# Stationary operands of the wide products stored with high and low words in turn

## The reference

```python
mix = jnp.einsum('btd,de->bte', merged, w_out[l])
...
h = h + _rmsnorm(jnp.einsum('btf,fd->btd', u, w_down[l]), post_mlp_norm[l])
...
def swiglu(x, w_gu, w_down):
    gu = jnp.einsum('bsd,df->bsf', x, w_gu)
    g, u = gu[..., :D_FF_2], gu[..., D_FF_2:]
    return jnp.einsum('bsf,fd->bsd', jax.nn.silu(g) * u, w_down)
...
    for e in range(N_EXPERTS):
        out = out + gates[..., e:e + 1] * swiglu(x, w_gu[e], w_down[e])
```

## Time and profile before

| | |
|---|---|
| median of 3 runs | 1770.74 us (1767.08 to 1770.81) |
| profiled execution | 1766.83 us, of it span 1765.0 us |
| PE busy | 1743.4 us, 99% |
| weight loads | 1571.6 us, 89% |
| DVE, ACT, POOL busy | 1361.9 us, 1076.1 us, 157.7 us |
| granted TensorE clock | 0.996 of full speed |
| read from HBM | 438.99 MB, 251 GB/s over the span |

### The profile page before, as it was taken

The page is one execution under the profiler, slowest core; times in us unless marked ns, Lnnn a source line. Parts: engine busy times, 40 slices in busy tenths (PEclk is TensorE's granted clock), DMA queues, the critical chain, the costliest instruction groups (busy, mean ns, idle before and its releaser), DMA issues.

```text
span 1765.0 us, 26513 instructions
## 1 busy us (share of the span) xinstructions
PE 1743.4 (99%) x11249; PEld 1571.6 (89%) x11249; DVE 1361.9 (77%) x1591; ACT 1076.1 (61%) x1200; POOL 157.7 (9%) x165
## 2 busy tenths in 40 slices
PE   9999999999999999999999999999999999999997
PEld 8999999999988999998998888888888888888885
DVE  6895488677764667656687899888889898889897
ACT  7654455565644454443446777777777777767674
POOL 1454170000000100000030100000000000000110
PEclk9999999999999999999999999999999999999999
DMA  9332364656556555565463699999999999999994
GB/s 290 120 109 72 118 176 136 226 180 194 192 188 203 193 172 172 183 228 187 128 225 112 232 376 378 378 342 384 369 385 339 383 371 383 333 379 375 381 390 171
DMA packets 265206, 447.90 MB, mean 254 GB/s; under 512 B 11461, under 2 KB 135848, under 8 KB 264952
## 3 DMA queue, kind: packets, MB, share of 16 engines
q1 hardware_dynamic: 263464, 440.36, 71.5%
q0 software_dynamic: 1616, 5.77, 0.8%
HBM read 438.99 MB, written 4.73 MB: 251 GB/s over the span
## 4 chain that ended last, share of the span: by engine, by line
PE 90%; DVE 6%; ACT 3%; issue 1%; DMA 0%; SPq 0%; DVEq 0%; ACTq 0%
PE bank L428 27%; PE bank L429 27%; PE bank L430 27%; DVE ring_r L418 3%; PE bank L3240 1%; ACT hi_ring L403 1%; PE bank L3154 1%; PE bank L2522 1%; PE bank L1348 1%; PE bank L1340 1%; DVE arena L923 1%; PE bank L1832 1%; PE bank L2503 0%; PE bank L2152 0%; PE bank L1817 0%
## 5 line engine op out<-in xcount | busy, mean ns | idle before, releaser
L418 DVE TENSOR_TENSOR ring_r<-ring,hi_ring 128x2048 fp32r<-128x2048 f32 x401 | 905.4, 2285 | 260.8 <-ACT hi_ring L403 260.5
L403 ACT CAST hi_ring<-ring 128x2048 fp32r<-128x2048 f32 (+1 forms) x404 | 757.3, 1904 | 133.1 <-PE bank L430 126.7
L428 PE MATMUL bank<-hi_ring,arena_r 128*128 128x512 f32 (+1 forms) x1526 | 568.5, 373 | 2.1 <-DVE ring_r L418 2.1
L429 PE MATMUL bank<-ring_r,arena_r 128*128 128x512 f32 (+2 forms) x1534 | 566.2, 369 | 0.0
L430 PE MATMUL bank<-hi_ring,arena_r 128*128 128x512 f32 (+1 forms) x1526 | 564.3, 370 | 0.0
L428 PE MATMUL bank<-ring_r,hi_ring 128*128 128x256 f32 (+1 forms) x1400 | 397.6, 284 | 0.3 <-DVE ring_r L487 0.3
L429 PE MATMUL bank<-ring_r,hi_ring 128*128 128x256 f32 (+1 forms) x1400 | 392.8, 281 | 0.0
L430 PE MATMUL bank<-ring_r 128*128 128x256 f32 (+1 forms) x1400 | 392.7, 280 | 0.0
L428 PEld LDWEIGHTS bank<-hi_ring,arena_r 128*128 128x128 f32 x1526 | 286.6, 188 | 54.0 <-DVE ring_r L418 4.9
L429 PEld LDWEIGHTS bank<-ring_r,arena_r 128*128 128x128 f32 (+1 forms) x1534 | 287.7, 188 | 48.9
L430 PEld LDWEIGHTS bank<-hi_ring,arena_r 128*128 128x128 f32 x1526 | 286.6, 188 | 50.0
(11 more groups left out here) (436 smaller groups left out, 1571.2 us busy)
## 6 DMA issues: line engine op xcount, KB each, us to landing
ring<-in_w_gu_moe SPq DMA_DIRECT2D x176, 1024.0 KB, 7.7
ring<-in_w_down_moe SPq DMA_DIRECT2D x88, 1024.0 KB, 6.4
ring<-in_w_in SPq DMA_DIRECT2D x31, 1024.0 KB, 5.5
ring<-in_w_gu_dense SPq DMA_DIRECT2D x22, 1024.0 KB, 5.1
ring<-in_w_up SPq DMA_DIRECT2D x16, 1024.0 KB, 5.6
ring<-in_w_down SPq DMA_DIRECT2D x16, 1024.0 KB, 5.0
ring<-in_w_in_a SPq DMA_DIRECT2D x10, 1024.0 KB, 5.8
ring<-in_w_down_dense SPq DMA_DIRECT2D x10, 1024.0 KB, 5.1
```

Of the source, the lines that this page charges most:

```text
L403: q.e.copy(hi_ring[:, b:b + m], ring[:, a:a + m]).then_inc(*q.did(("hi", of.tag, i)))
L418: q.e.tensor_tensor(ring_r[:, a:a + m], ring[:, a:a + m], hi_ring[:, b:b + m].bitcast(F32), ALU.subtract).then_inc(*q.did(("lo", of.tag, i)))
L428: q.e.matmul(ps, a[0], b[0], start=first, stop=False)
L429: q.e.matmul(ps, a[0], b[1], start=False, stop=False)
```

## The change

A new class, Woven, holds one of the two words of an operand in a piece of memory where high and low words lie in turn: word 2i is the high and word 2i + 1 the low part of element i. Reads and writes of either part then step by 8 bytes instead of 4. The operands mg, u_, mix2, gg, xs2 and hp are made with it. All of them and ST begin 16 words earlier in the arena (at 8 modulo 64 words, which is 128 bytes from the weights modulo 256); hh, which lies between xs2 and hp, moves along. The helpers act_turn and dve_turn no longer flatten hp, as the new class gives flat rows itself. Products, their order, waits and DMAs are as before.

```diff
--- before.py
+++ after.py
@@ -178,6 +178,22 @@
         self.hi, self.lo = hi, lo
 
 
+class Woven:
+
+
+    def __init__(self, a, tiles, part):
+        self.tiles, self.n = tiles, a.shape[1] // (2 * tiles)
+        self.words = a.rearrange("p (n h) -> p n h", h=2)[:, :, part]
+
+    def __getitem__(self, at):
+        _, k, cols = at
+        a, b = cols.start or 0, cols.stop or self.n
+        if isinstance(k, slice) and b - a < self.n:
+            return self.words.rearrange("p (k n) -> p k n", k=self.tiles)[:, k, a:b]
+        k0, k1 = (k.start, k.stop - 1) if isinstance(k, slice) else (k, k)
+        return self.words[:, k0 * self.n + a:k1 * self.n + b]
+
+
 class Weights:
 
 
@@ -277,6 +293,10 @@
     def pair_at(o, *dims):
         n = int(np.prod(dims))
         return Pair(at(o, *dims, of=arena_r), at(o + n, *dims, of=arena_r))
+
+    def woven_at(o, tiles, n):
+        a = at(o, 2 * tiles * n, of=arena_r)
+        return Pair(Woven(a, tiles, 0), Woven(a, tiles, 1))
 
     def flat(a):
         return a.rearrange("p a b -> p (a b)")
@@ -545,11 +565,11 @@
     swapped |= {("aq", j): at(SEQ * j, SEQ) for j in range(8)}
     rel = [at(17584 + T * j, T) for j in range(3)]
     gate_a, gate_b = at(20656, 8, SEQ), at(0, 8, SEQ)
-    mg, xin2 = pair_at(13016, 8, SEQ), at(17152, 2, 1024)
+    mg, xin2 = woven_at(13000, 8, SEQ), at(17152, 2, 1024)
     mix, n2, mix_gain = at(6528, 2, 1024), at(8576, 2, 1024), at(19200, 1024)
     mix_junk, x2_junk, qx2 = at(10624, 256), at(10880, 512), [at(11648 + SEQ * j, SEQ) for j in range(4)]
     mix_sq, x2_sq, r_mix, r_x2 = at(12672, 2, 4), at(12680, 2, 2), at(12684, 2), at(12686, 2)
-    u_, dn = pair_at(2072, 32, SEQ), at(18456, 2, 1024)
+    u_, dn = woven_at(2056, 32, SEQ), at(18456, 2, 1024)
     ut = [at(18456 + SEQ * j, SEQ) for j in range(4)]
     dn_gain, dn_junk, dn_sq, r_dn = at(21272, 1024), at(21016, 256), at(22296, 2, 4), at(22304, 2)
 
@@ -563,7 +583,7 @@
     kms = [shaped(C[:, late + 512 * j:late + 512 * j + 512], (2, SEQ)) for j in range(2)]
     vms = [shaped(C[:, o:o + 520], (2, 4, 65)) for o in (late + 1024, later)]
     cos2, sin2 = C[:, later + 520:later + 776], C[:, later + 776:later + 1032]
-    mix2 = pair_at(6616, 8, SEQ)
+    mix2 = woven_at(6600, 8, SEQ)
     kx, vx = at(10752, 6, SEQ), at(12288, 2, 12 * 65)
     memT, memin = pair_at(22328, 8, SEQ), at(2176, 2, 1024)
     mk_raw = [at(2048, 8, P), at(14368, 8, P)]
@@ -576,7 +596,7 @@
     qx = at(14368, 6, SEQ)
     swap2 = {"kx": at(22376, 6, SEQ), "qx": at(23912, 6, SEQ)}
     swapped |= {(name, j): swap2[name][:, j, :] for name in swap2 for j in range(6)}
-    gg = pair_at(6616, 22, SEQ)
+    gg = woven_at(6600, 22, SEQ)
     gtmp = [at(17920 + SEQ * j, SEQ) for j in range(4)]
 
     xt = [pair_at(4096 + 2048 * c, 1024) for c in range(2)]
@@ -585,9 +605,9 @@
     lgT = at(8344, SEQ)
     pm = at(8600, 2, 2 * P, of=arena_r)
     gs = at(9112, 8)
-    ST = [at(9624 + 256 * j, SEQ, of=arena_r) for j in range(4)]
-    xs2 = pair_at(10648, 8, 2 * P)
-    hh, hp = at(14744, 2816), pair_at(17560, 22, P)
+    ST = [at(9608 + 256 * j, SEQ, of=arena_r) for j in range(4)]
+    xs2 = woven_at(10632, 8, 2 * P)
+    hh, hp = at(14728, 2816), woven_at(17544, 22, P)
     acc, moe_gains = at(2048, 2, 1024), at(0, 2, 1024)
     lparts, lmv, linv = at(9128, 24), at(9152, 4), at(9156, 2)
     wsum, wbias, shift = small(8), small(8), small(2)
@@ -3242,11 +3262,11 @@
 
     def act_turn(q, R, x, f):
         n = turned(f) * P
-        act_split(q, flat(hp.hi[:, f:f + turned(f), :]), R.banks(R.tag, "turn", x, f)[:, 0:n], ("ps", R.tag, "turn", x, f), ("hphi", R.tag, x, f))
+        act_split(q, hp.hi[:, f:f + turned(f), :], R.banks(R.tag, "turn", x, f)[:, 0:n], ("ps", R.tag, "turn", x, f), ("hphi", R.tag, x, f))
 
     def dve_turn(q, R, x, f):
         n = turned(f) * P
-        dve_split(q, flat(hp.hi[:, f:f + turned(f), :]), flat(hp.lo[:, f:f + turned(f), :]), R.banks(R.tag, "turn", x, f)[:, 0:n], ("hphi", R.tag, x, f), ("hp", R.tag, x, f))
+        dve_split(q, hp.hi[:, f:f + turned(f), :], hp.lo[:, f:f + turned(f), :], R.banks(R.tag, "turn", x, f)[:, 0:n], ("hphi", R.tag, x, f), ("hp", R.tag, x, f))
         R.banks.drop((R.tag, "turn", x, f), ("hp", R.tag, x, f))
 
     def pe_up(q, R, x):
```

## The result

| | before | after |
|---|---|---|
| median of 4 runs | 1769.66 us (1767.08 to 1770.81) | 1780.37 us (1778.97 to 1782.44) |
| profiled execution, its span | 1766.83 us, 1765.0 us | 1781.45 us, 1779.6 us |
| ratio to before | | 1.0064, 95% interval 1.0048 to 1.0080 |

The change makes the kernel slower, by 0.64%. The time lies in the range, but the forecast of 1735 us had the wrong sign: 35 us of gain were expected, and 11 us were lost.

A forecast was written before the change was run, and what follows sets the result against it. PE was taken as the bound, through the number and spacing of mm3's matmuls. From a median of 1770.7 us, 33.5 us (512 columns) and 1.7 us (256 columns) came off: 1735.5, stated as 1735 us, range 1718 to 1795.

The forecast's parts named there:

- The stationary step: mm3's 512-column products, with loads stepping 8 bytes: spacing from 229.0 to 219.9 ns, 3,678 products, 33.5 us gained.
- the whole extra: 512-column products in mm3: 15.7 ns of spacing beyond the 213.3 ns of their columns, supposed to be collisions of two reads.
- The 6.6 ns: Smallest extra seen on 256-column products, taken as what load and stream still cost each other once a load at 512 columns.
- 256-column products: Experts' last up-product chunk and row products' split last bank, 852 products: 2 ns less each, 1.7 us gained.
- Offsets at nothing: Six groups of arrays and their neighbours move down 16 words in the arena; claimed to cost nothing.
- Writes: ACT's and DVE's casts and subtractions into the woven arrays, writing every second word; claimed to cost nothing.
- the 13 us bound: Worst case for the pick copies on ACT and DVE, doubled in time with no PE work to hide under.
- Supply: DMA feeding a pair of experts: needs 382 GB/s after the change, against 388 GB/s once moved; claimed to just hold.
- Rival B: In the experts, DMA sustains no more than 375 GB/s and takes part of the gain: 1749 us, chance 0.14.
- C: mm3's products: extra belongs to the 4-byte stream or handing over, not addresses; nothing changes, 1767 to 1774 us, chance 0.12.
- D: mm3's loads touch twice as many memory pieces, each holding up the stream: 1804 to 1838 us, chance 0.26.
- A's range: The forecast's own case, mm3's extra shrinks and DMA keeps up: 1716 to 1752 us, chance 0.48.

The follow-up runs named there:

- the benches: PE alone runs groups of 48 products, one form each, with the reference's work left out; contiguous 512-column products at distance 48 words took 229.0 ns each.

## Why the prediction was wrong

**What bounds the kernel.** Right. PE sets the end in both, the clock is 1.00, DMA takes no part (the benches have none), and no wait came or went.

**The stationary step, 220 ns: the step that failed.** It measured 231.5 ns, 2.4 more instead of 9.1 less: +8.8 us where -33.5 stood. The premise was that the whole extra is a meeting of two reads, which a fixed distance at equal rate avoids, down to 6.6 ns. Two things were wrong in it. First, 13.4 of the 15.7 ns stay in fp32r wherever the loads are: the best of all groups is 226.7 ns, with both operands in bf16 it is 215.6. For 512 columns this alone leaves 2.4 ns to win. The 6.6 ns, taken over from 256 columns, were about half of what 512 columns keep at their best. The trace of before held signs of it: 272 columns had an extra of 12.5 ns and the pick 13.0, and at a granted clock of 0.50 the extra of 256 columns was nothing. Second, a fixed distance finds no free lane: woven loads give 230.0 to 233.5 ns at all eight distances. Contiguous ones range wider, from 226.7 to 234.2, and before was at 229.0.

**256-column products.** Predicted -2 ns, measured +3.6: 3.1 us lost instead of 1.7 gained. In the bench step 2 gives 120.0 ns at almost any distance, near the top of what step 1 gives.

**Offsets at nothing.** True for the number of instructions, false for the time: with contiguous operands the new offsets cost 3.5 ns a product by themselves. The prediction had the distance as part of the meeting, but never gave the old distance a value of its own to lose. That the whole change lost only 2.4 is no merit of the weave in general: at distance 32 a woven load happens to be 1.0 ns better than a contiguous one.

**Writes.** Right. ACT +26 ns and DVE +5 ns for each copy, hidden; the 13 us bound wasn't needed.

**Supply.** Never tested, since PE didn't get faster. Rival B is not refuted. The 191.1 us taken for a pair were a window 0.8 us longer than a pair.

**The rivals.** C is right for most of the extra, in that it does not go by addresses. Of its two causes, a fixed time for the handing over does not fit the lower clock (no extra for 256 columns); the stream of 4-byte words fits, but stream and load were never changed apart. Its result was wrong, since the rest does depend on addresses. D had the sign: it was to decide "where the interval ends above 229", and it ended at 231.5, far under its 237. Its mechanism, a price for each piece of memory a load touches, holds only in part. At equal distance a woven load costs 6.6 ns more at 0 and 4.3 more at 48, but 3.3 less at 16 and 1.0 less at 32, and loads of a quarter of the columns are not cheaper. Steps of 3 and 4 words are dearer at all four places tried.

**Small slips in the sums.** Half of the gain taken is 17.6 us, so the end of A's range was 1753 and not 1752, and the 10.8 ns for the worst case of 256 columns stand on no row. Neither changes the forecast.

**The pages.** The rule of the Trainium skill, "TensorE: Matmul & The Clock Gate", Step-by-step: what each phase is for, that loading takes no bandwidth from the running matmul, was nearest in size. It leaves out 2 to 7 ns that step, distance and place do decide. The rule of the Trainium skill, "SBUF — State Buffer", Specifications (TRN2), on lines of 16 bytes spoke for the right sign. The runs agree with it where a load has one word in each line (step 4: 235.0 to 239.6 ns). At two words in a line they show both signs, by distance.

**Still open.** Why fp32r products need at least 13 ns over their columns' time at a granted clock of 1.00 (512 columns), and 256 columns none at 0.50, whether load or stream brings this, and what chooses between two states of one form. All were seen, none explained.

## What to carry to other kernels

Where all the time is in one form of instruction, run that form by itself with the suspected cost taken away (another type, a quarter of the load, one address) before building on it: a floor of 226.7 ns would have shown that 2.4 ns were to be had and not 16. Don't carry an extra from one width to another; look at several widths, and at a stretch of the other clock if the trace has one. Move operands against each other by whole offsets and measure step and distance as a pair, since the two parts of this change cost 4.2 and 3.5 ns alone and 2.4 together. A placement that helps one width can cost another its gain, so use it where the first outnumbers the second.

## What the runs showed of the hardware

- fp32r products of 512, 384, 320, 272 and 256 columns have their best spacing in the benches at 226.7, 173.3, 146.7, 125.4 and 113.3 ns (384 and 272 were tried at two distances, 320 at one); bf16 has 215.6 for 512 and 109.2 for 256. At a granted clock of 0.50, fp32r with 256 columns has 213.3, without an extra. Settled fp32r spacings are often whole multiples of 6.67 ns (16 cycles at the granted 2.4 GHz): 17, 18, 34 and 35 of them. Values between are patterns over several products, as the period of seven after.
- One form with one set of addresses has two stable spacings, 113.3 or 117.8 ns for 256 columns, 230.0 or 233.3 for woven loads at distance 16, and can keep one for 86 us (256 columns) or 330 us (woven, 512). In the profiled execution of before this was worth 2.4 us, more than half of the 3.5 us that distance 0 in the experts gains.
- The spacing repeats with 64 words of distance: 226.7 ns at 0 and 64, 229.0 at 48 and 112. At distance 0 it also goes by where the stream begins: 226.7 ns at five places that are multiples of 8 words, 230.0 and 233.3 at 36 and 44 words modulo 64.
